# Norm scales moved behind the products, and dilated attention beside them, in a three-block transformer step

## The reference

```
# block 1: RWKV-7 mixer and chunked attention
h = rms_norm(x, pre_norm_g);  proj = h @ w_in
y_r = rwkv7(h, p_r, p_k, p_v, low-rank projections of h mixed with h of the token before) * silu(z_r)
y_a = chunk_band_attention(q, k, v, rel_bias) * silu(z_a)
o = (sigmoid(m_r + b0) * (y_r @ w_branch_rwkv) + sigmoid(m_a + b1) * (y_a @ w_branch_attn)) @ w_out
x = x + rms_norm(o, post_norm_g)
# block 2: top-k attention and a spatial gating unit, then an MLP
proj = rms_norm(x, norm1_g) @ w_in_2
x = x + (sigmoid(ga) * sparse_attention(...) + sigmoid(gb) * sgu(gelu(u), gelu(v))) @ w_out_2
x = x + square(relu(rms_norm(x, norm2_g) @ w_ff1)) @ w_ff2
x = rms_norm(x, final_g)
# block 3: pooling mixer and dilated attention of 8 heads of 128, then an MLP
proj = rms_norm(x, norm_mix_g) @ w_in_3            # u (1024), q, k, v (1024 each)
y = concat(rms_norm(pool_mixer(u), pool_out_norm_g), rms_norm(dilated_attention(q, k, v), attn_out_norm_g))
x = x + y @ w_out_3
x = x + square(relu(rms_norm(x, norm_mlp_g) @ w_up)) @ w_down
return rms_norm(x, norm_final_g)
```

## Time and profile before

| | before |
|---|---|
| median of 3 runs | 3885.57 us |
| the profiled execution | 3883.54 us |
| its span | 3881.8 us |
| mean granted TensorE clock | 0.948 |
| PE busy | 3639.1 us (94%) |
| DVE busy | 2130.2 us (55%) |
| ACT busy | 1552.3 us (40%) |
| POOL busy | 28.4 us (1%) |
| DMA | 591.46 MB, mean 152 GB/s |

### The profile page before, as it was taken

How to read it: one execution, slowest core, us unless ns; L and a number is a source line. 1 busy time by engine, 2 the same in 40 slices (tenths; PEclk the granted TensorE clock), 3 DMA queues, 4 the chain that set the end, 5 groups by cost and what they waited for, 6 DMA issues and landing times.

```text
span 3881.8 us, 53665 instructions
## 1 busy us (share of the span) xinstructions
PE 3639.1 (94%) x22881; PEld 3128.7 (81%) x22881; DVE 2130.2 (55%) x3118; ACT 1552.3 (40%) x1981; POOL 28.4 (1%) x115
## 2 busy tenths in 40 slices
PE   7999989989979999999899999997995999999998
PEld 6887877777868877878788888887873888888887
DVE  4456655456646465556565456544543556546544
ACT  2454333324423445434344444433332434444432
POOL 1000000000000000000000000000000000000000
PEclk8999999999979999999899999997995989999998
DMA  5554323225524644535466566662550546666652
GB/s 159 175 168 146 126 96 99 97 80 181 185 81 147 195 141 141 163 121 183 132 193 186 185 188 188 188 186 87 177 169 1 174 141 185 190 188 186 188 188 91
DMA packets 586198, 591.46 MB, mean 152 GB/s; under 512 B 20758, under 2 KB 581222, under 8 KB 585447
## 3 DMA queue, kind: packets, MB, share of 16 engines
q1 hardware_dynamic: 585960, 588.04, 48.7%
HBM read 581.68 MB, written 6.32 MB: 151 GB/s over the span
## 4 chain that ended last, share of the span: by engine, by line
PE 87%; DVE 8%; ACT 2%; issue 1%; DMA 1%; SPq 0%; DVEq 0%; ACTq 0%
PE gp L1960 49%; PE gp L1966 26%; PE sidep L896 4%; PE sidep L430 3%; DVE w_parts L1895 2%; ACT w_parts L1888 1%; DVE high L449 0%; DVE low L449 0%; PE sidep L1415 0%; ACT lo_half L1644 0%; PE sidep L1414 0%; PE sidep L1115 0%; DMA high<-bias_rows 0%; PE sidep L435 0%; PE sidep L1109 0%
## 5 line engine op out<-in xcount | busy, mean ns | idle before, releaser
L1895 DVE TENSOR_TENSOR w_parts<-ring,w_parts 128x1024 fp32r<-128x1024 f32 x1084 | 1326.7, 1225 | 1076.9 <-ACT w_parts L1888 1075.7
L1888 ACT ACTIVATE w_parts<-ring 128x1024 fp32r<-128x1024 f32 x1084 | 1145.3, 1057 | 1228.3 <-PE gp L1966 1228.2
L1960 PE MATMUL gp<-x_parts,w_parts 128*128 128x512 f32 x6112 | 1601.6, 402 | 35.2 <-DVE x_parts L459 13.3
L1960 PEld LDWEIGHTS gp<-x_parts,w_parts 128*128 128x128 f32 x6112 | 1111.5, 192 | 246.8 <-issue 27.3
L1966 PEld LDWEIGHTS gp<-x_parts,w_parts 128*128 128x128 f32 x6112 | 833.2, 192 | 63.9 <-issue 4.4
L1966 PE MATMUL gp<-x_parts,w_parts 128*128 128x256 f32 x6112 | 873.5, 286 | 1.7 <-DVE w_parts L1895 1.7
L1960 PE MATMUL gp<-ff_parts,w_parts 128*128 128x512 f32 x2560 | 649.2, 395 | 0.0
L1960 PEld LDWEIGHTS gp<-ff_parts,w_parts 128*128 128x128 f32 x2560 | 459.2, 188 | 87.4
L1966 PEld LDWEIGHTS gp<-ff_parts,w_parts 128*128 128x128 f32 x2560 | 350.5, 188 | 29.5
L1966 PE MATMUL gp<-ff_parts,w_parts 128*128 128x256 f32 x2560 | 358.7, 282 | 0.0
L1644 ACT ACTIVATE lo_half<-gp 128x512 f32<-128x512 f32 x247 | 147.6, 598 | 482.9 <-PE gp L1966 482.9
(11 more groups left out here) (334 smaller groups left out, 1660.9 us busy)
## 6 DMA issues: line engine op xcount, KB each, us to landing
ring<-w_in SPq DMA_DIRECT2D x220, 1024.0 KB, 5.2
ring<-w_ff SPq DMA_DIRECT2D x128, 1024.0 KB, 5.6
ring<-w_up SPq DMA_DIRECT2D x64, 1024.0 KB, 5.7
ring<-w_down SPq DMA_DIRECT2D x64, 1024.0 KB, 5.4
ring<-w_out SPq DMA_DIRECT2D x48, 1024.0 KB, 5.5
ring<-w_branch_rwkv SPq DMA_DIRECT2D x8, 1024.0 KB, 5.5
ring<-w_branch_attn SPq DMA_DIRECT2D x8, 1024.0 KB, 5.5
gate_scratch<-stage SPq DMA_DIRECT2D x16, 256.0 KB, 2.0
```

The lines of the kernel that those rows point to most:

```text
L1888: act.activation(w_parts[:, q % PARTS, 0], ring[:, u % RING, SLOT * (q % 2):SLOT * (q % 2) + SLOT, :], ACT.Copy).then_inc(high_split, 1)
L1895: v.tensor_tensor(w_parts[:, q % PARTS, 1], ring[:, u % RING, SLOT * (q % 2):SLOT * (q % 2) + SLOT, :], w_parts[:, q % PARTS, 0].bitcast(F ...
L1960: pe.matmul(gp[:, k % 2, j, :, :], w_parts[:, q % PARTS, 0, c, j * P:(j + 1) * P], operand(s, b, SLOT * n + c), start=(n == 0 and c == 0), ...
```

## The change

What it does, in the order of time:

- **Norms.** x itself, times gain, is split into halves, two chunks at a time, as the residual sums of the section before come in (`next_norm`: out2, down2_1, out3a). The product of the next section is then made of unscaled x, and 1/rms multiplies each block's sums after the evacuation: one more DVE operation of 128x512 in each of 191 blocks (`scaled_by`, `block_scaled`), ahead of what used them. ACT squares each block's chunks as they come, POOL adds the squares up (`Rms.add`), and PE sums two tiles instead of all chunks, some slots into the next section.
- **final2 and mix3** become one: the squares are taken twice, without and with final2's gain, and both inverse roots come from one run; final2's scaling of `xt` goes beside in3.
- **post and norm1**: o1 is squared and gained block by block beside out; after the last block DVE multiplies by 1/rms, POOL adds into `xt`, ACT and DVE make the halves, four chunks at a time.
- **Start**: x in four loads, halves made per two chunks as they are turned, 1/rms from ACT's squares of the rows with an accumulator; the parameters are loaded after the first two weight loads. The low-rank projections use x and are scaled afterwards.
- **Block 3**: in3's columns are ordered so that q, k, v of a pair of heads come in three blocks in a row; dilated attention runs in two chains beside in3 and the first half of out3, one pair in 12 slots. out3 is split in two sections of 8 blocks of two slots, out3p (pooled half, scaled by its own 1/rms) and out3a (attention half), with halves of y made as heads end. That is 8 blocks more and no slot more.
- **End**: final3's gain is applied and x turned block by block beside down3_1; after the last root ACT and DVE scale the rows, and eight stores of 256 KB follow.

The core of the diff:

```diff
-        section("in3", 16, 16, columns(w3, 0))
-        section("out3", 8, 16, columns(I["w_out_3"][0], 0))
+        section("in3", 16, 16, lambda b, r: [(piece(w3, r * UNIT * P, in3_chunk(b) * P), 0, NB)])
+        section("out3p", 8, 8, columns(I["w_out_3"][0], 0))
+        section("out3a", 8, 8, columns(I["w_out_3"][0], 0, POOLED))
...
+        def split_low_gained(v, g, gain, high):
+
+            v.wait_ge(x_high_split, high)
+            for c in range(2 * g, 2 * g + 2):
+                m = v.scalar_tensor_tensor(x_parts[:, c, 1, :], xt[:, c, :], gains(gain, c),
+                                           x_parts[:, c, 0, :].bitcast(F32), ALU.mult, ALU.subtract)
+            m.then_inc(x_split, 1)
...
+            def add(self, pool, b):
+                if 1 <= b < self.blocks - 1:
+                    pool.wait_ge(self.squared, b + 1)
+                    if b > 1:
+                        pool.wait_ge(self.added, b - 1)
+                    for k in range(self.sets):
+                        m = pool.tensor_tensor(self.acc[k], self.acc[k], self.sq[b - 1][k], ALU.add)
+                    m.then_inc(self.added, 1)
...
+                elif s.name in next_norm:
+                    norm, gain, _ = next_norm[s.name]
+                    act.wait_ge(finished, fin_count(s.name, b))
+                    for n in (2 * b, 2 * b + 1):
+                        m = act.activation(x_parts[:, n, 0, :], xt[:, n, :], ACT.Copy, scale=gains(gain, n))
+                    m.then_inc(x_high_split, 1)
+                    norm.square(act, b, xt[:, c, :], lambda i: par("final2", 2 * b + i))
...
+                v.tensor_tensor(to, gp[:, k % 2, :, 0, :], lo_half[:, k % 2], ALU.add).then_inc(block_evacuated, 1)
+            late = 2 if s.name == "index2" and b == 0 else 1
+            if s.name in scaled_by and phase == late:
+                v.wait_ge(block_evacuated, k + 1)
+                v.tensor_tensor(to, to, over(scaled_by[s.name], 2), ALU.mult).then_inc(block_scaled, 1)
+                v.wait_ge(block_scaled, scaled(s.name, b))
...
+            scale(0)
+            scale(1)
+            low_halves(0)
+            scale(2)
+            low_halves(1)
+            scale(3)
+            yield 0.34
+            low_halves(2)
+            yield 0.67
+            low_halves(3)
...
+        norm_after("out2", "norm2", [rstd])
+        norm_after("down2_1", "gain_23", [variance, rstd], 2)
...
+        first_pair = at("in3", 7) + 0.5
         att3 = [Attention3(th) for th in range(2)]
         for th in range(2):
-            att3[th].thread(at("out3"), 0.0)
+            att3[th].thread(first_pair + 0.5 * th, 0.6)
...
+        norm_after("out3a", "mlp3", [rstd])
+        final3 = Rms("final3", 8, 2, low, 8192, None)
+        threads.append(Thread("turn", at("down3_1", 1) + 2.0, 1.0, tensor=turn_tensor, scalar=turn_scalar, vector=turn_vector, sync=store_sync))
...
-                    if b == 0 and s.name in x_ready:
-                        pe.wait_ge(x_split, x_ready[s.name] + n + 1)
+                    if b == 0 and halves_ready(s.name, n) is not None:
+                        pe.wait_ge(x_split, halves_ready(s.name, n))
```

More of the change, by code:

```diff
@@ L33 @@
 HEADS2, KV2 = 16, 4
+POOLED = 1024
 FAR, TAKEN = -1.0e38, -3.0e38
@@ L218, in block_end, with scaled, over @@
             return S[name].slot0 + (b + 1) * S[name].slots
-        def summed(name, b):
-            return S[name].block0 + b + 1
+        scaled_by, scaled0, n_scaled_blocks = {}, {}, 0
+        for s in order:
+            if s.name not in ("branch", "out", "out2", "down2_0", "down2_1", "down3_0", "down3_1"):
+                scaled_by[s.name] = {"out3p": variance_t}.get(s.name, rstd)
+                scaled0[s.name] = n_scaled_blocks
+                n_scaled_blocks += s.blocks
+        def scaled(name, b):
+            return scaled0[name] + b + 1
+        def over(tile, n):
+            return tile[:, 0:TOK].rearrange("p (o t) -> p o t", o=1).to_broadcast([P, n, TOK])
         rows, row_list = {}, []
@@ L1486, in pool_pool @@
                     pool.wait_ge(counts_made, n)
+            for g in range(1, 3):
+                yield 11
+                pout.add(pool, g)
         def pool_vector(v):
@@ L1809, in build_kernel @@
         mer_split = Split(mer, 16, mer_ready, 0, 0.5, ff_parts).thread("merged", at("branch", 4) + 0.67, at("branch", 4) - at("branch"))
-        post = Norm(o1, DC, "post", area(high, 0, DC), "add",
-                    after=lambda act: act.wait_ge(block_evacuated, summed("out", 7))).thread("post", at("index2"))
-        norm1 = Norm(xt, DC, "norm1", area(high, 0, DC), "split", area(high, 4096, DC), free=S["out"].end,
-                     after=lambda act: act.wait_ge(n_stored, 4)).thread("norm1", at("index2"))
@@ L1837, in build_kernel, with norm_after @@
-        mix3 = Norm(xt, DC, "mix3", area(high, 0, DC), "split", area(high, 4096, DC), free=S["up2_1"].end,
-                    after=lambda act: act.wait_ge(n_scaled, final2.scaled0 + DC)).thread("mix3", at("in3") + 0.34)
+        next_norm = {}
+        def norm_after(name, gain, dst, sets=1):
+            norm = Rms(gain, 8, 2, low, 4096, dst, sets)
+            next_norm[name] = (norm, gain, counts["xs"])
+            counts["xs"] += 8
+            return norm.thread(gain, S[name].end, (1.34, 1.67, 2.67, 3.0))
@@ L1851, in build_kernel @@
-        threads.append(Thread("store", n_slots + 1, 0, tensor=store_tensor, vector=store_vector, sync=store_sync))
-        x_ready = {"qkv": pre.xs0, "index2": norm1.xs0, "up2_0": norm2.xs0, "in3": mix3.xs0, "up3_0": mlp3.xs0,
-                   "out": mer_split.xs0, "out2": merged2_split.xs0}
+            att3[th].thread(first_pair + 0.5 * th, 0.6)
+        aout = Rms("aout", 8, 1, low, 8704, [rstd])
+        threads.append(Thread("ya", first_pair + 7.0, 1.0, scalar=ya_scalar, vector=ya_vector, gpsimd=ya_pool))
@@ L1856, in operand @@
+        before_section = {"up2_0": "out2", "in3": "down2_1", "up3_0": "out3a"}
         def operand(s, b, c):
@@ L2010, in _ @@
                     side.run(q + 0.67)
-                side.run(n_slots + 1)
+                side.run(n_slots + 9)
 def kernel(**inputs):
```

614 lines of the change are left out of this document (407 added, 207 removed).

## The result

| | before | after |
|---|---|---|
| median | 3885.24 us (3880.71 to 3887.41, 4 runs) | 3730.22 us (3724.54 to 3734.39, 4 runs) |
| profiled execution, span | 3881.8 us | 3732.7 us |
| ratio | | 0.9602 [0.9584, 0.9619] |

Forecast were 3653 us and a range of 3613 to 3698; measured 3730. The sign was right, and 155 of the 233 us that were forecast came.

What follows compares the result with a forecast made beforehand. The chain was 87% PE: long stretches of products with holes of 342.6 us in all. Gains 17 + 34 + 24.5 + 48 + 74 + 25.5 + 22 less 12 gave 233, so 3653 us, range 3613 to 3698.

Steps and rivals of the forecast that it cites:

- The multiplications: 191 multiplications by 1/rms on DVE: nothing without side work; 12 us lost beside it, between bounds of 0 and 45.
- Rival A: In za, gates, zr, ga2, gb2 ACT waits 1.9 us longer a block for scaled sums: +38, 3691 us; chance 0.13.
- The shared port: DVE stands while GpSimd adds: 4 to 8 us in out3a, some 3 in index2's hole, giving 3662; chance 0.1.
- Column sums: PE's sums of squares in norms: 0.20 us each at the lower clock, 0.12 at the upper; index2's hole, 8 sums 1.7.
- up2_0: Hole ahead of up2_0 goes, as halves are made while out2's sums come; 1.5 us added on PE: gain 24.5.
- The end: After the last product: a tail of 13 us instead of 38, 3 us of transposes beside products: gain 22.
- Block 3: in3, out3 and up3_0: gains of 48, 74 (attention beside products, out3 in two halves) and 25.5, 147.5 together.
- out3a's order: In out3a, order rather than load gives rounds of 7.1 us for 5.66 of products: 10 us lost over eight blocks.
- The start: First product at 21.5 us instead of 43.6, PE waiting 2.4 for the root inside slot 0: gain 17.
- E: Rival: a hole stays because a norm's 1/rms or a half comes late, one or two of 25 us: 3690; chance 0.06.
- D: Rival: DVE becomes the bound, PE waiting 1.93 us at each of 191 blocks: 4010 us, slower; chance 0.02.

Runs made afterwards that it cites:

- e2: Changed kernel with a memset of one column in place of each of the 191 multiplications by 1/rms, order and waits kept: 3686.1 us.
- e3: Changed kernel with a memset of one column in place of each multiplication by 1/rms, right after the block's addition: 3678.5 us.
- e9: Changed kernel with each multiplication by 1/rms made twice, one behind the other: 3797.65 us.
- e1: Changed kernel with DVE's multiplication by 1/rms right after the block's addition, ahead of side work and weight split (index2's first block excepted): 3722.9 us.
- e4: Changed kernel with ACT waiting for the multiplication only in the five sections where it reads the result: 3720.5 us.
- e5_pool_tiny: Changed kernel with GpSimd's additions of squares and post norm's four additions to x replaced by memsets of one column: 3716.28 us.
- e6: Changed kernel with out3a's squares behind the next weight split, and norm sums one slot later in up2_0, in3, up3_0: 3724.38 us.
- e10: Changed kernel with e1, e4, e6 and e7 together, lora thread at slot 6, and all index2 additions on DVE: 3689.02 us.
- e7: Changed kernel with ACT's row squares behind the first two weight splits, the root later, lora arithmetic 2.5 slots later: 3722.15 us.
- e8_mult_pool: Changed kernel with all 191 multiplications by 1/rms on GpSimd, ACT waiting only where it reads the result: 3728.94 us.

## Why the prediction was off, point by point

**The multiplications, -12 forecast, 41 measured by their duration, and this is the step that failed.** "PE is busy 387 of 420 us in gates, so most is covered: I take 12", out of bounds of 0 and 45 for the sections with side work. The busy share of PE says how long the products and side matmuls take, and nothing of whether DVE's next step was awaited. e2, e3, the changed kernel and e9 show that in gates it was: at least a us for each us added. The upper bound was the near one: in the seven sections it was made for, e2 gives back 34 us by the duration alone and e3, with the order, 45, and e9 adds 48. It was a bound that the text itself had worked out and then discounted by the wrong row. The sections without side work were put at nothing, and za and up2_1 bear that out. For in3 the text had no such price, and for out3 one in its rounds; e2 gives back 3.7 and 5.8 there.

**Rival A** had the place and the wait right (37.4 us of ACT's waiting in gates, 25 gone in e1) and the price wrong: 38 by the rival, 5 measured for the order (e1), 8 for dropping the wait where ACT needs no result (e4).

**The shared port**, named as rule and rival with 9 us, is real. With the latency of the additions in the chain it costs 11 us by the ratio (e5_pool_tiny), and it lies elsewhere: "4 to 8 us" in out3a are 1.6, "some 3" at index2 are 10.7 behind the first product. There it meets instructions of 0.47 us that last 2.6 each; in out3a it meets five weight splits, which last 1.63 us for 1.21.

**Column sums.** "8 sums 1.7" in index2's hole counts too few: the kernel issues eight sums there and the trace has sixteen matmuls, two for each sum in f32, and the 0.20 us from "12.88 over 64" is that of one of the two. The sixteen take 3.26 us at index2 in this profile and 3.55 at the end; at a granted clock of 1.00 they take 1.92, which would have hidden the slip. The terms of up2_0, in3 and up3_0 have both the count and the upper clock: 1.92 us for 1.0, 4.69 (32 records, clock 0.77) for 1.9 and 3.54 (clock 0.50) for 1.0. The end is 17 us long for 13 forecast, 2.3 of these by the sums.

**Block 3**, 131.7 for 147.5. Of the missing 16, e3 gives back 6 and e6 some 6 (in3's 2.6 among them, which e10 leaves open). out3a's order was foreseen well: a round of 7.2 us in the trace for 7.1 in the text, its eight blocks 51 us for 55. That in3 carries the pooling mixer, the attention and sixteen scalings at 2.8 us a head could not be split further; the rest, some 4 to 7 us, stays open.

**The start**: first product 23.5 for 21.5, because ACT had all 3.8 us of row squares ahead of the first weight split; and 10 us lost in qkv, of which the forecast knew the root's 2.4 and not the lora's steps behind a late load. Counting from the first product, e7 gives back 5 us of the start and qkv together, and e10 8.

**Still open**: 14 of the 57 us that neither order nor duration gives back, a size that is as rough as single profiles are. The largest piece is qkv2, which is 6.7 us longer in e3 than in the kernel before. 3.4 of these are in view in the changed kernel: in qkv2 index selection waits at once for index2's last multiplication (PE 1.2 us) and then for a DVE step that stands behind a weight split (2.2).

**The signs.** "Wrong if gates grows by over 20, if one of the other holes stays at 10 or more, or if in3 and out3p together take over 280": gates grew by 15.5, no hole stayed, and in3 and out3p took 277.8. None of the three spoke, and the time still lay outside the range: the sign for gates, 20, was wider than the whole term of 12 that it was to watch. What was to be seen if the forecast held, "gates within 10 us of 420", was missed with 434.4.

**Right**: up2_0 within 1.2 us; no hole left (E), DVE not the bound (D); GpSimd's addition of 128x1024 at 2.3 to 2.6 for 2.2. PEclk was to be 1.00 at the first products of up2_0, in3 and up3_0; it is in the first of them alone:

```profile
1930.70:1940.00 9.30, 9.30 (x58) 7.91 (x56) 6.53 (x19) 4.98 (x7) 1.14 (x9) 1.00 0.62 189
2653.10:2662.00 8.90, 8.13 (x52) 7.30 (x51) 4.62 (x6) 4.72 (x8) 3.81 (x30) 0.90 0.39 120
2981.90:2991.50 9.60, 4.12 (x23) 3.12 (x21) 6.84 (x11) 4.47 (x9) 1.45 (x1) 0.81 0.59 169
```

In up3_0 PE is busy 4.1 of 9.6 us: out3a's last block comes late, and the sums of squares, placed inside slot 1, wait for its square. Of the hole that left the section's head, 5 us came back inside it, and the whole section is 9.3 us longer than before.

## What to carry over

An engine that is busy 55% of a stretch can still set its length: where two chains of small steps alternate between engines, price added work there at its full duration (here 34 to 48 us for 44 of work), and let only an experiment (a tiny instruction in its place, and the work done twice) talk it down. An engine that is idle is not free either when it shares a port: 131 us were taken off DVE, and its splits grew by 135. Keep GpSimd's additions away from stretches in which DVE issues many short instructions with two SBUF inputs.

## What the runs showed of the hardware

- GpSimd's tensor_tensor with no DVE instruction ahead of it: 128x512 in 1.29 us, 128x1024 in 2.35; 1.36 (120 of them, e8_mult_pool) and 2.54 to 2.64 in the mean, with those that waited. DVE takes 0.69 and 1.22.
- A DVE instruction with two SBUF inputs that starts during one ends a fixed time after it, 0.28 us for 128x256 (2.6 for 0.47) and 1.08 for 128x1024 (2.25 for 1.23 beside 128x512; 169 of them). When DVE's has started first, GpSimd's 128x512 takes 2.20 for 1.29 (24). A DVE instruction with one input in PSUM isn't lengthened: 0.41 beside one as alone.
- A sum over partitions of one f32 column shows as two matmuls, 0.20 us each at a granted clock of 0.55, 0.12 at 1.00.
- The same matmuls of gates keep PE busy 387.8 us at a granted clock of 0.95 and 395.4 at 0.93.
